# Padding the 64 sample rows to 128 in the recurrent stage of a two-layer decoder step

## The reference

```
d      = exp(log_d - m_t)                      # decay between tokens, causal
s      = (q k^T) * d
num    = s v + inter * (C0 q)                  # C0: carried state, one per sample sequence
den    = sum(s) + inter * (n0 . q)
h      = num / max(|den|, exp(-m_t))
w_last = d[last token]
C_new  = decay * C0 + (v * w_last)^T k         # per sequence
n_new  = decay * n0 + w_last . k
```

## Time and profile before

| | |
|---|---|
| median of 3 runs | 1299.93 us (1297.12 to 1302.91) |
| the profiled execution | 1296.63 us |
| its span | 1295.3 us |
| TensorE busy | 1218.9 us (94%) |
| VectorE, ScalarE, POOL busy | 582.2, 397.9, 144.7 us |
| mean granted TensorE clock | 0.981 |

### The profile page before, as it was taken

The page is one execution under the profiler, slowest core; times in us unless marked ns, Lnnn a source line. Parts: engine busy times, 40 slices in busy tenths (PEclk is TensorE's granted clock), DMA queues, the critical chain, the costliest instruction groups (busy, mean ns, idle before and its releaser), DMA issues.

```text
span 1295.3 us, 20873 instructions
## 1 busy us (share of the span) xinstructions
PE 1218.9 (94%) x8548; PEld 741.8 (57%) x8548; DVE 582.2 (45%) x1163; ACT 397.9 (31%) x739; POOL 144.7 (11%) x179
## 2 busy tenths in 40 slices
PE   6999999999999799998998998999999799999996
PEld 5866678777776433333336776776777454333332
DVE  3754467576544722222126567536554551221212
ACT  3533423244442211111125334445444311111112
POOL 5210022111001010100001131001000101100100
PEclk9999999899999899999999999989999999999999
DMA  9575353366767379999984476713765948999994
GB/s 301 164 216 160 98 163 112 108 213 248 252 249 326 150 303 422 420 420 421 421 311 131 148 251 241 251 39 98 293 261 195 362 158 347 406 421 420 421 418 176
DMA packets 114028, 340.52 MB, mean 263 GB/s; under 512 B 7598, under 2 KB 75514, under 8 KB 86272
## 3 DMA queue, kind: packets, MB, share of 16 engines
q1 hardware_dynamic: 108752, 323.51, 66.5%
q0 software_dynamic: 4736, 14.42, 3.6%
q10 hardware_dynamic: 432, 1.11, 0.2%
HBM read 328.48 MB, written 10.54 MB: 262 GB/s over the span
## 4 chain that ended last, share of the span: by engine, by line
PE 80%; DMA 7%; DVE 6%; ACT 4%; issue 2%; POOL 1%; SPq 0%; DVEq 0%; POOLq 0%; ACTq 0%
PE ps L2356 15%; PE ps L614 9%; PE ps L615 9%; PE ps L616 9%; PE ps L2431 6%; DMA arena<-in_w_exp_up 6%; PE ps L2400 4%; PE ps L1517 3%; PE ps L1531 2%; PE ps L1556 2%; PE ps L1620 2%; PE ps L1602 2%; DVE wl L608 2%; PE ps L2334 1%; PE ps L854 1%
## 5 line engine op out<-in xcount | busy, mean ns | idle before, releaser
L2356 PE MATMUL ps<-arena,mkv 128*64 128x512 f32 x1024 | 225.8, 593 | 8.3 <-DMA arena<-in_w_exp_up 7.6
L614 PE MATMUL ps<-bx,wh 128*128 128x320 f16 (+2 forms) x688 | 193.4, 289 | 10.1 <-DVE wl L608 4.1
L615 PE MATMUL ps<-bx,wh 128*128 128x320 f16 (+2 forms) x688 | 193.3, 288 | 0.0
L616 PE MATMUL ps<-bx,wl 128*128 128x320 f16 (+2 forms) x688 | 193.0, 288 | 0.0
L608 DVE SCALAR_TENSOR_TENSOR wl<-stg,wh 128x1024 f16<-128x1024 f32 x122 | 152.6, 1290 | 51.9 <-ACT wh L600 51.9
L600 ACT ACTIVATE wh<-stg 128x1024 f16<-128x1024 f32 x122 | 122.4, 1050 | 148.2 <-PE ps L616 130.2
L2356 PEld LDWEIGHTS ps<-arena,mkv 128*64 128x64 f32 x1024 | 75.5, 137 | 152.6 <-issue 150.9
L2571 DVE TENSOR_TENSOR arena<-ps,arena 128x512 f16<-128x512 f32 x64 | 44.1, 689 | 160.6 <-ACT arena L2517 113.5
L614 PEld LDWEIGHTS ps<-bx,wh 128*128 128x128 f16 x688 | 68.9, 101 | 36.0 <-issue 14.2
L2575 DVE COPY arena<-ps 128x1 f32<-128x1 f32 x32 | 5.1, 159 | 184.4 <-PE ps L2378 184.4
L614 PE MATMUL ps<-arena,wh 128*128 128x320 f16 x288 | 86.6, 301 | 0.9 <-ACT mkv L1199 0.9
(11 more groups left out here) (433 smaller groups left out, 1789.0 us busy)
## 6 DMA issues: line engine op xcount, KB each, us to landing
arena<-in_w_exp_gate SPq DMA_DIRECT2D x60, 1024.0 KB, 12.0
arena<-in_w_exp_up SPq DMA_DIRECT2D x60, 1024.0 KB, 14.0
arena<-in_w_exp_down SPq DMA_DIRECT2D x32, 1024.0 KB, 14.7
stg<-in_w_exp_down SPq DMA_DIRECT2D x32, 1024.0 KB, 16.1
arena<-in_cache_mem_k SPq DMA_DIRECT2D x16, 1024.0 KB, 8.0
arena<-in_cache_mem_v SPq DMA_DIRECT2D x16, 1024.0 KB, 5.0
stg<-in_w_in_a SPq DMA_DIRECT2D x28, 512.0 KB, 4.7
stg<-in_w_qkv_c SPq DMA_DIRECT2D x20, 512.0 KB, 4.0
```

The costliest lines, as they stand in the source:

```text
L614: nc.tensor.matmul(out, wh[:, s, at:at + 128], hi, start=start, stop=False, **flags)
L615: nc.tensor.matmul(out, wh[:, s, at:at + 128], lo, start=False, stop=False, **flags)
L616: return nc.tensor.matmul(out, wl[:, s, at:at + 128], hi, start=False, stop=stop, **flags)
L2356: last = nc.tensor.matmul(ps[64 * j:64 * j + 64, UB, :], xe[:, q % 2, j, k, :], gu[:, g % 2, j, :, k, :], start=(k == 0), stop=(k == KD - ...
```

## The change

The rows 64 to 127 of tile 2 in `ktok`, `vtok`, `dmat` and `wlast`, and of `vw`, are set to zero by POOL, and the products that read them take all 128 rows. There are two new blocks of memsets on POOL, a semaphore `row_pad`, and new waits for it on TensorE and POOL. VectorE and ScalarE go on writing rows 0 to 63 alone.

```diff
 # mlstm_pool
         for h in range(2):
             pool.dma_start(state(h), ...).then_inc(slot_in[h], 16)
+        pool.wait_ge(S["w_lo"], 2 * max(AHEAD) + 2)
+        pool.wait_ge(S["acc_ready"], ADDS[1])
+        rows = slice(64, 128)
+        nc.gpsimd.memset(ktok[rows, 2, :], 0.0)
+        nc.gpsimd.memset(vtok[rows, 2, :], 0.0)
+        nc.gpsimd.memset(dmat[rows, :, 384:448], 0.0)
+        nc.gpsimd.memset(wlast[rows, :, 0:8], 0.0).then_inc(S["row_pad"], 1)
         pool.wait_ge(S["rows_ready"], 1)
...
         pool.wait_ge(S["ei_ready"], HA)
+        pool.wait_ge(S["row_pad"], 1)
         decay(0)
         pool.wait_ge(S["w_ev"], sum(UNIT["in_b"]))
+        pool.wait_ge(S["decay_ready"], 1)
+        nc.gpsimd.memset(vw[rows], 0.0).then_inc(S["row_pad"], 1)
+        pool.wait_ge(S["row_pad"], 2)
         pool.wait_ge(S["ml_ev"], 1)
 # numerators(h)
                 pe.wait_ge(S["s_ready"], HA)
+                pe.wait_ge(S["row_pad"], 1)
...
-                    lhs = vtok[0:n, tile, 128 * h:128 * h + 128] if left is None else ones[0:n, :]
-                    nc.tensor.matmul(ps[:, bank, t0:t0 + w], lhs, dmat[0:n, h, c:c + w], start=first, stop=False,
+                    lhs = vtok[:, tile, 128 * h:128 * h + 128] if left is None else ones[:]
+                    nc.tensor.matmul(ps[:, bank, t0:t0 + w], lhs, dmat[:, h, c:c + w], start=first, stop=False,
 # updates(h)
             if h == 0:
                 pe.wait_ge(S["w_ev"], UK)
+                pe.wait_ge(S["row_pad"], 2)
...
-                nc.tensor.matmul(ps[:, 4 + b // 4, 128 * (b % 4):128 * (b % 4) + 128], vw[0:64, b, :],
-                                 kt[0:64, 2, :], start=True, stop=True)
+                nc.tensor.matmul(ps[:, 4 + b // 4, 128 * (b % 4):128 * (b % 4) + 128], vw[:, b, :],
+                                 kt[:, 2, :], start=True, stop=True)
...
-            nc.tensor.matmul(ps[:, 2, 128:136], kt[0:64, 2, :], wlast[0:64, h, 0:8], start=True, stop=True)
+            nc.tensor.matmul(ps[:, 2, 128:136], kt[:, 2, :], wlast[:, h, 0:8], start=True, stop=True)
```

More of the change, by code:

```diff
@@ L353, in build @@
         ml_ev cleared xt_ps xt_hi xt_lo pt_ev pk_ready gate_lo xg_ps xg_act xg_dve z_ps
-        zs_act zs_dve zt_ps qd_ready kt_act kt_dve bs_ps bo_ps bo_ev qp_ready padded id_in mem_hi hsum_ev""".split()
+        zs_act zs_dve zt_ps row_pad qd_ready kt_act kt_dve bs_ps bo_ps bo_ev qp_ready padded id_in mem_hi hsum_ev""".split()
     S = {n: sem(n) for n in names}
```

## The result

| | before | changed |
|---|---|---|
| median | 1299.93 us (1297.12 to 1302.91) | 1285.44 us (1284.15 to 1287.50), 5 runs each |
| ratio | | 0.9887, 95% interval 0.9862 to 0.9913 |
| profiled execution, its span | 1296.63, 1295.3 us | 1284.15, 1282.8 us |

The changed kernel is 1.1% faster; forecast were 1287.4 us and, for the profiled execution, 1284.1. Its lines have moved: L1062, L1067, L1084, L1088 are now L1074, L1079, L1097, L1101, and VectorE's L1306 and L1316 are L1319 and L1329. In this trace the first part of the program, up to L1308 of head 0, ran 0.8 us later than in the trace of before, so lengths of stretches are compared and not times of day. (In the thirteen traces of this document that point lies between 188.5 and 190.8 us.)

A forecast was written before the change was run, and what follows sets the result against it. TensorE was taken to bound the kernel, with 80% of the chain that ended last. Savings of 3.15 (head 0), 6.5 (heads 1 and 2) and 2.8 (head 3), together 12.5 us, gave 1287.4 from 1299.9; range 1280.5 to 1294.

The forecast's parts named there:

- Price of the padded pair: TensorE's updates, L1084: a 128-row pair costs 0.22 us, as at L1088, with bounds of 0.14 and 0.42.
- rival A: Updates on TensorE: the 64-row pair's length is not the row-shape switch's; only 4.4 us go, 1295.5; 12 in 100.
- What a crossing costs: TensorE's passage between 128-row and 64-row products around L1084: 0.10 us going in, about 0.20 coming out.
- Numerators: L1062's two groups of six passes on TensorE: padding saves 0.34 and 0.41 us, together 0.75 a head.
- Tail: End of a head's updates, L1089 between L1088 and L1091: 1.31 us becomes 1.1, saving 0.2 a head.
- POOL: POOL's two memset blocks: the first costs nothing inside idle time, the memset of vw makes TensorE wait 0.1 us.
- VectorE next: VectorE is late next: just covered in heads 1 and 2; in head 3 only 2.04 us until L1316 can go.
- Low clock in head 3: 1.2 GHz stretch of 6.8 us behind TensorE's wait for L861: stays, and costs at most 3.4 us.
- rival D: The low clock of head 3 goes as well: 1284 us, within the forecast; 15 in 100.
- The sum: Recurrent stage: 3.15 us in head 0, 6.5 in heads 1 and 2, 2.8 in head 3, together 12.5.
- Rival B: VectorE comes last in each head; a slip of 1 us a head takes 4 of the 12.5: 1291.5; 15 in 100.
- rival C: POOL's vw memset is kept off by VectorE; TensorE idles 5.5 us, the clock falls, 13.6 lost: 1301; 3 in 100.

The follow-up runs named there:

- 64-row updates: Changed kernel with the products of the updates (L1084, L1089) back at 64 rows, numerators still padded: 1291.78 us, ratio to before 0.9951.
- groups of two: Kernel before, its 64-row L1084 products standing in twos with the fill's steps behind each two: 1294.70 us, ratio to before 0.9960.
- kernels with late keys: Changed kernel with keys(1) behind numerators(3) on TensorE and outputs(3) on VectorE: 1281.85 us; with VectorE's fill(5) behind keys(2) too: 1281.56 us.
- late memset: Changed kernel with POOL's memset of vw moved behind the convolution inputs: 1293.43 us, ratio to before 0.9955.
- groups of eight: Kernel before, a head's eight 64-row L1084 products in a row and the fill's eight steps behind them: 1294.21 us, ratio to before 0.9957.

## Why the prediction was right, step by step

- **Price of the padded pair** (0.22 from L1088): 0.23. The bounds of 0.14 and 0.42 were not needed, and the 0.42 to 0.44 of rival A did not come. The period of 0.55 and the updates of 5.5 us came as forecast.
- **What a crossing costs** (0.10 in, 0.20 out): 0.10 and 0.19, shown by the two kernels with grouped 64-row products, without any padding.
- **Numerators** (0.34 and 0.41 a head): 0.33 and 0.43. The six passes take 0.82 and 0.83 (0.85 forecast, from the two lengths in the earlier trace rows) and the L1067 pair behind the first six 0.20 (0.16): two small errors of opposite sign.
- **Tail** (0.2): 0.29, since the L1102 pair with 8 columns takes 0.14 and not 0.22; this was put too low by 0.1 a head.
- **POOL**: nothing and 0.1 forecast; nothing and at most 0.06 measured. The memset took 0.94 beside VectorE's split, at the price of a memset elsewhere. So the stretched L934 was no guide to a memset, and L934 itself went from 4.39 to 3.40. The rule of the Trainium skill ("SBUF — State Buffer", Who interferes with whom) that the prediction cites frees a GpSimd instruction that only writes SBUF from this contention; the trace agrees with it, 0.94 us beside the split.
- **VectorE next**: heads 1 and 2 just covered, as forecast, and thinner than thought: 0.18 us idle were left in head 2 and not 0.55, since the split beside POOL took 3.70 (3.26 before). In head 3 the add comes 5.92 behind the outputs, 8.09 before, 2.17 saved; 2.04 was forecast.
- **Low clock in head 3**: left in its place, and it stayed in both traces, in one of them with half its length. Its price was put at up to 3.4 us; measured are 3.1 for 6.8 us. That rival D, that it goes, did not come is chance as much as mechanism: in two of the traces with this wait (64-row updates, groups of two) the clock stayed full behind it. The kernels with late keys bring rival D about on purpose.
- **The sum**: 12.5 forecast, 12.64 in the stage, 12.5 between the two spans. That the profiled execution came out at 1284.15 against 1284.1 is in part luck: it is the fastest of its five, and the 0.8 lost ahead of the stage and 0.6 gained behind it happen to cancel. The medians differ by 14.5, 2 us more. In the second traces, too, the difference (12.2 us, 1297.12 to 1284.95) is that of the sum. Of the other 2 us one is the median of before, which was 1298.75 and 1298.95 in the two larger sets; the rest lies within what executions of one kernel differ by, and its cause stays open.

Rival B did not come, but only by 0.2 us of idle time on VectorE in head 2. POOL was not late, so rival C did not come, and its price was put too high: the late memset made TensorE wait 5.96 us (5.5 in rival C), but the low clock behind it covered only 6 us of work where rival C had all of the updates and the fill behind them at half speed, so that the stage lost 9.3 and not 13.6. Even then the kernel was faster than before (1293.43 against 1298.75), not slower.

## What to carry to other kernels

Look in TensorE's timeline for short idle times put down to "issue" where the row shape of products changes (`64*128` beside `128*128`), and count the crossings, not the small products: each pair cost 0.30 us here, and either padding with zeros or putting the products of one shape in a row removes it. Here a padded product was no dearer than the small one, and that could be read beforehand: the 128-row form of the same product stood in the same trace with its price. Before padding, find the engine that must write the zeros, when it can, and who waits behind it: the late memset took back 9.3 of the 12.6 us.

## What was not expected of the hardware

TensorE's clock fell in the two kernels with grouped products while the engine was busy without a gap: from 189.4 us in the one with groups of eight, 187.9 in the other, while the 64-row products of head 0 ran, with the sixteen passes of 8 columns before them. For the second (groups of two), windows of 3 us:

```profile
186.00:189.00 3.00, 3.00 (x18) 0.81 0.41 131
189.00:192.00 3.00, 3.00 (x13) 0.50 0.64 218
...
201.00:204.00 3.00, 3.00 (x16) 0.50 0.39 112
```

It stayed low for 17.1 us of unbroken work. Up to the first pair of head 0's updates the products ahead of it are those of the kernel before, whose two traces show full clock there. In that same trace the 2.44 us of waiting for L861 brought no fall, as in one trace of the kernel with 64-row updates; in the other traces with that wait one of 3.4 to 6.8 us came each time. Which of them comes in an execution is not settled here. It makes single executions of one kernel differ by 3 us and more, so a difference of 3 us between two medians is no proof of an edit's worth; the length of a head, which repeats to 0.01 us, is.
